# Order of the vector work in two attention layers: an eviction moved inside a head, copies, reciprocals and selection rounds moved between steps

## The reference

```python
# first layer, per block of 128 queries and head (16 heads of 64)
z = einsum(q, k) * scale
log_fail = where(mask, log_sigmoid(-z), 0.0)
later = cumsum(log_fail, reverse=True) - log_fail
a = where(mask, exp(log_sigmoid(z) + later), 0.0)
out = einsum(a, v)                      # then * silu(gate), @ w_out

# even layer: 8 heads of selected-key attention, 8 heads with three branches
rel = relu(einsum(q_idx, k_idx)); score = einsum(w_idx, rel)     # masked
_, idx = top_k(score, 128)              # topk = min(256, 512 // 4)
p = masked_softmax(einsum(q, k[idx]) * scale, valid)             # "d" units
# compressed keys ("c" units), selected blocks and window ("n" units)
o = g[..., 0] * o_c + g[..., 1] * o_s + g[..., 2] * o_w
```

## Time and profile before

| | |
|---|---|
| median of 3 runs | 2005.2 us (2001.36 to 2007.17) |
| the profiled execution | 2002.36 us, of it 2000.6 us span of the instructions |
| mean granted TensorE clock | 0.966 |
| PE busy (matmuls) | 1873.5 us, 94% |
| DVE, ACT, POOL busy | 49%, 40%, 24% |
| first layer's attention rounds | about 127 to 320 us |
| even layer: projections, then steps | about 616 to 732, 732 to 950 us |

### The profile page before, as it was taken

How to read it: one execution, slowest core, us unless ns; L and a number is a source line. 1 busy time by engine, 2 the same in 40 slices (tenths; PEclk the granted TensorE clock), 3 DMA queues, 4 the chain that set the end, 5 groups by cost and what they waited for, 6 DMA issues and landing times.

```text
span 2000.6 us, 24568 instructions
## 1 busy us (share of the span) xinstructions
PE 1873.5 (94%) x9662; PEld 1482.6 (74%) x9662; DVE 981.2 (49%) x1591; ACT 799.8 (40%) x1407; POOL 480.3 (24%) x478
## 2 busy tenths in 40 slices
PE   6999988997999889889999999999999899999997
PEld 5987776774577746656788888887877688888885
DVE  5345554587445566653543333355555454333334
ACT  4235554336434354435443233242444344332322
POOL 0035551000312344423021111003566302110100
PEclk9999999998999988979999999999999799999999
DMA  4321111221012410000233232222111023223232
GB/s 158 96 74 43 43 43 42 85 86 51 1 32 92 130 56 22 22 11 12 85 95 104 88 104 95 96 94 74 54 54 52 22 85 106 95 95 106 90 101 74
DMA packets 40289, 143.32 MB, mean 72 GB/s; under 512 B 4592, under 2 KB 4976, under 8 KB 40176
## 3 DMA queue, kind: packets, MB, share of 16 engines
q1 hardware_dynamic: 40176, 141.76, 21.9%
HBM read 139.64 MB, written 2.10 MB: 71 GB/s over the span
## 4 chain that ended last, share of the span: by engine, by line
PE 82%; DVE 8%; ACT 5%; issue 2%; POOL 2%; DMA 0%; DVEq 0%; SPq 0%; ACTq 0%; POOLq 0%
PE BANK L268 21%; PE BANK L270 21%; PE BANK L269 20%; PE BANK L832 2%; PE BANK L1458 1%; PE BANK L1415 1%; PE BANK L617 1%; DVE LH L703 1%; PE BANK L1439 1%; DVE SCR L698 1%; ACT WH L245 1%; PE BANK L886 1%; PE BANK L602 1%; PE BANK L2187 1%; PE BANK L2134 1%
## 5 line engine op out<-in xcount | busy, mean ns | idle before, releaser
L245 ACT ACTIVATE WH<-WRAW 128x1024 fp32r<-128x1024 f32 x262 | 273.3, 1045 | 473.6 <-PE BANK L270 430.9
L268 PE MATMUL BANK<-HH,WH 128*128 128x512 f32 x1048 | 428.1, 408 | 30.2 <-DVE WL L254 18.1
L254 DVE TENSOR_TENSOR WL<-WRAW,WH 128x1024 fp32r<-128x1024 f32 x242 | 318.9, 1318 | 255.2 <-ACT WH L245 255.0
L270 PE MATMUL BANK<-HL,WH 128*128 128x512 f32 x1048 | 412.1, 393 | 0.0
L269 PE MATMUL BANK<-HH,WL 128*128 128x512 f32 x1048 | 411.9, 393 | 0.0
L268 PEld LDWEIGHTS BANK<-HH,WH 128*128 128x128 f32 x1048 | 199.0, 190 | 80.9 <-issue 22.2
L269 PEld LDWEIGHTS BANK<-HH,WL 128*128 128x128 f32 x1048 | 199.0, 190 | 43.4 <-issue 5.3
L270 PEld LDWEIGHTS BANK<-HL,WH 128*128 128x128 f32 x1048 | 198.8, 190 | 42.7
L2075 POOL TENSOR_TENSOR HID<-TMP,HID 128x512 fp32r<-128x512 f32 x64 | 82.7, 1293 | 526.9 <-ACT HID L2056 526.9
L268 PE MATMUL BANK<-HID,WH 128*128 128x512 f32 x512 | 199.2, 389 | 0.0
L269 PE MATMUL BANK<-HID,WL 128*128 128x512 f32 x512 | 199.2, 389 | 0.0
(11 more groups left out here) (373 smaller groups left out, 3217.0 us busy)
## 6 DMA issues: line engine op xcount, KB each, us to landing
WRAW<-in_w SPq DMA_DIRECT2D x77, 512.0 KB, 3.4
WRAW<-in_wu SPq DMA_DIRECT2D x64, 512.0 KB, 3.3
WRAW<-in_wd SPq DMA_DIRECT2D x64, 512.0 KB, 3.3
WRAW<-in_w0o SPq DMA_DIRECT2D x8, 512.0 KB, 3.5
WRAW<-in_w1o SPq DMA_DIRECT2D x8, 512.0 KB, 3.4
WRAW<-in_wc SPq DMA_DIRECT2D x8, 512.0 KB, 3.3
WRAW<-in_w2o SPq DMA_DIRECT2D x8, 512.0 KB, 3.3
WRAW<-in_w3o SPq DMA_DIRECT2D x8, 512.0 KB, 3.4
```

Source lines behind the costliest of these rows:

```text
L245: e.activation(WH[b % NS][:, 0:n], WRAW[b % NR][:, 0:n], ACT.Copy).then_inc(*inc("s_high", ("high", b)))
L254: e.tensor_tensor(WL[b % NS][:, 0:n], WRAW[b % NR][:, 0:n], WH[b % NS][:, 0:n].bitcast(F32), ALU.subtract).then_inc(*inc("s_low_pool" if p ...
L268: e.matmul(dst, ah, bh, start=first and i == 0, stop=False)
L270: made = e.matmul(dst, ah, bl, start=False, stop=last and i == len(sets) - 1)
```

## The change

In the first layer `taken` is cut into `evicted` and `high`. The eviction of the first tile beside the heads stands behind the first cut of the second head's `fails`; `gated` goes behind that head, and the tile's high plane and the weight split behind `gated`. In the even layer four weight blocks (tiles 5 to 8) leave `on_pool` and are split by DVE. The rounds ahead of the steps are 5 + 5 instead of 4 + 3 + 3, and the third `index_sum` stands behind the eviction of tile 8. In the steps ACT copies ahead of the exponentials; reciprocals and scales come one step later; DVE's rope sum, ACT's high and POOL's low part of a turned tile come one step later, with POOL's cosine ahead of its scale. The rounds are one in a step in which a tile is turned, added or evicted and in every odd step, and two in the others; what is left is made in step 34.

```diff
-                   if block["e", 5] <= b <= block["e", 14] + NS and name not in ("wc1", "wc2")
+                   if block["e", 9] <= b <= block["e", 14] + NS and name not in ("wc1", "wc2")
...
             for m in range(8):
                 fails(2 * m)
+                fails(2 * m + 1, [0])
+                beside = l0_beside[m]
+                if len(beside) > 0:
+                    evicted(*beside[0])
+                fails(2 * m + 1, [1, 2])
                 if m:
                     gated(m - 1)
-                fails(2 * m + 1)
-                for t in l0_beside[m]:
-                    taken(*t)
+                if len(beside) > 0:
+                    high(*beside[0])
+                if len(beside) > 1:
+                    evicted(*beside[1])
+                    high(*beside[1])
...
             rounds = e_rounds(e, w)
-            for _ in range(4):
+            split("wc1", 1, 2)
+            for _ in range(5):
                 next(rounds)
-            split("wc1", 1, 2)
...
-            for _ in range(3):
+            for _ in range(5):
                 next(rounds)
             taken(E_Q)
             split("e", E_Q)
             after_rope(E_KW)
             keys(1)
-            index_sum(3)
             after_rope(E_Q)
-            for _ in range(3):
-                next(rounds)
             taken(E_Q + 1)
             split("e", E_Q + 1)
             c_keys(1)
             split("wc2", 1)
+            index_sum(3)
             for step in range(E_STEPS):
                 if 0 <= step - 1 < E_N:
                     maxima(step - 1)
-                if 0 <= step - 2 < E_N:
-                    recips(step - 2)
+                if 0 <= step - 3 < E_N:
+                    recips(step - 3)
...
+                if e_turning(step - 1) is not None:
+                    roped(e_turning(step - 1))
                 if e_turning(step) is not None:
-                    after_rope(e_turning(step))
+                    sines(e_turning(step))
...
-                next(rounds, None)
-                if step == e_first[4] - 3:
+                busy = [t for t in (e_turning(step - 1), e_turning(step), e_ended(step)) if t is not None]
+                for _ in range(1 if busy or step % 2 else 2):
+                    next(rounds, None)
+                if step == e_first[4] - 2:
                     for _ in rounds:
                         pass
...
             for step in range(E_STEPS):
-                if 0 <= step - 1 < E_N:
-                    exps(step - 1)
...
                 if 0 <= step - E_TURN < E_N:
                     copied(step - E_TURN)
-                if e_turning(step) is not None:
-                    high(e_turning(step))
+                if 0 <= step - 1 < E_N:
+                    exps(step - 1)
+                if e_turning(step - 1) is not None:
+                    high(e_turning(step - 1))
...
             gelu_low(1)
-            split("e", E_Q)
             cos(E_Q)
             low(E_Q)
+            split("e", E_Q)
             split("e", E_Q + 1)
             split("wc2", 1)
             w.wait_ge(*at("gates"))
             for step in range(E_STEPS):
-                if 0 <= step - 2 < E_N:
-                    scale(step - 2)
                 if e_turning(step) is not None:
                     cos(e_turning(step))
-                    low(e_turning(step))
+                if 0 <= step - 3 < E_N:
+                    scale(step - 3)
+                if e_turning(step - 1) is not None:
+                    low(e_turning(step - 1))
                 if e_ended(step) is not None:
                     split("e", e_ended(step))
```

More of the change, by code:

```diff
@@ L676, in l0_vector, with evicted @@
                 split_low(e, w, after_block(("l0v", b), 1), False)
-            def taken(name, m):
+            def evicted(name, m):
                 q = name == "l0q"
-                t = TMP[:, 2 + (not q), :]
                 w.wait_ge(*at("tile", name, m))
@@ L684, in taken, with high @@
                     w.wait_ge(*at("l0 low", name, m - 1))
-                e.scalar_tensor_tensor(out=t, in0=banks[name, m], scalar=0.125 if q else 1.0, in1=RS[:, :], op0=ALU.mult,
-                                       op1=ALU.mult).then_inc(*inc("s_evac", ("evac", name, m)))
+                e.scalar_tensor_tensor(out=TMP[:, 2 + (not q), :], in0=banks[name, m], scalar=0.125 if q else 1.0,
+                                       in1=RS[:, :], op0=ALU.mult, op1=ALU.mult).then_inc(*inc("s_evac", ("evac", name, m)))
+            def high(name, m):
+                q = name == "l0q"
                 w.wait_ge(*at("evac", name, m))
@@ L689, in taken, with fails @@
                     w.wait_ge(*at("z", 2 * m - 3, 2))
-                e.tensor_copy(l0_plane(m, 0 if q else 2), t).then_inc(*inc("s_l0_high", ("l0 high", name, m)))
+                e.tensor_copy(l0_plane(m, 0 if q else 2), TMP[:, 2 + (not q), :]).then_inc(
+                    *inc("s_l0_high", ("l0 high", name, m)))
                 split_low(e, w, after_block(name, m), False)
-            def fails(h):
+            def fails(h, ks=range(3)):
                 v = l0_buf[h % 3]
-                for k in range(3):
+                for k in ks:
                     c = cuts[k]
@@ L712, in gated @@
                     *inc("s_gated", ("gated", m)))
[L713 to L714 removed]
+            for t in l0_first:
+                evicted(*t)
+                high(*t)
             for m in range(8):
                 fails(2 * m)
+                fails(2 * m + 1, [0])
[3 more added lines that the diff above has]
+                fails(2 * m + 1, [1, 2])
                 if m:
                     gated(m - 1)
[L719 to L721 removed]
+                if len(beside) > 0:
[3 more added lines that the diff above has]
+                    high(*beside[1])
             gated(7)
@@ L1561, in after_rope, with sines @@
             def after_rope(t):
+                sines(t)
+                roped(t)
+            def sines(t):
                 w.wait_ge(*at("e rot", t))
```

1 line of the change is left out of this document (added).

## The result

The changed kernel takes **1978.2 us** (median of 4 runs, 1970.64 to 1981.56) against 2006.2 us (4 runs, 2001.36 to 2010.72) before: ratio 0.9855, 95% interval 0.9818 to 0.9893. Run again, beside 7 more runs of the kernel before, it gave 1977.5 us, ratio 0.9829 (0.9801 to 0.9857). The profiled execution took 1976.83 us, with 1975.0 us of span, at a mean granted clock of 0.970; the one of before took 2002.36 us.

What follows compares the result with a forecast made beforehand. Matmuls filled 94% of the span, leaving PE's idle and below-full-clock time to win. Terms -8.1 - 3.6 + 2.5 - 2.2 - 11.4 = -22.8 us gave 1979.6, or 1982 us on the median's footing; range 1974 to 1991.

Steps and rivals of the forecast that it cites:

- First layer, -8.1: First layer: five PE waits of 1.69 us for the eviction go, 0.3 us lost in the last round; -8.1 us.
- Head of the even layer, -3.6: Ahead of the steps: first scores 4.6 us sooner, some given back by the first turn; -3.6 us.
- `index_sum` and two rounds now lie ahead of the first maxima: Head of the even layer: one reason why part of the 4.6 us won at the first scores is given back.
- Turned tiles, +2.5: Steps: waits for cosine, scale and DVE, 15.7 us, replace 13.2 us of waits for copies; +2.5 us.
- The moved rope sum: Turned tiles: sum kept at 0.69 us; by the rule up to one `scale` lost at each of seven, 10 us.
- Late maxima, -2.2: Steps: at the 3.8 us wait, reciprocal and `scale` end near 848.0 instead of PE's restart at 850.12; -2.2 us.
- End of the selection, -11.4: Burst of rounds spread out: wait -6.3, lower clock behind it -4.6, shorter drop -0.5; -11.4 us.
- Rival 1: Turned tiles cost little: six waits of 2.5 us halve and the clock stays at 2.4 GHz; 1970 us, chance 0.15.
- rival 4: Nothing moves: first layer's wait goes over to `sums`, turned tiles eat the rest; 2000 to 2008 us, chance 0.08.
- Rival 3: Turned tiles: split, cosine and scale in line on GpSimd make waits of 5.1 us; 2016 us, chance 0.12.
- Rival 2: Steps 18 to 31: DVE becomes the bound through long rounds and the moved sum; 1994 us, chance 0.15.
- just fits: Steps: with reciprocals a step later, maxima, reciprocal and scale take 2.9 us against steps of 2.6 to 4 us.

Runs made afterwards that it cites:

- e1: The kernel before with only the first layer's part of the change; 1997.5 us, ratio 0.9942 to before.
- e6: The changed kernel with ACT's exponentials ahead of the copies again, as before the change; 1983.3 us, ratio 0.9884 to before.
- e4: The changed kernel with the third `index_sum` back ahead of the query's rope; 1971.2 us, ratio 0.9819 to before.
- e9: The changed kernel with reciprocals and scales a step sooner, third `index_sum` back, GpSimd's scale ahead of the cosine; 1945.8 us, ratio 0.9674 to before.
- e2: The changed kernel with the old order of the first layer, so only the even layer's part; 1988.3 us, ratio 0.9912 to before.
- e3: The changed kernel with GpSimd's scale ahead of the cosine in each step; 1966.1 us, ratio 0.9801 to before.
- e10: The kernel before with only the new pattern of selection rounds; 1997.3 us, ratio 0.9937 to before.
- e5: The changed kernel with one selection round a step and the rest at once in step 33; 1983.8 us, ratio 0.9879 to before.
- e7: The changed kernel with reciprocals and scales a step sooner, as before, cosine still ahead of scale; 1954.7 us, ratio 0.9739 to before.
- e11: The changed kernel with reciprocals and scales a step sooner and the third `index_sum` back; 1941.7 us, ratio 0.9647 to before.

## Why the prediction was right, and where it was not

The forecast of 1982 us lies 4 us over the result, and the range holds it. The nearness is partly luck: the trace has +8.1 us in the latent layer and -3.1 us behind the even layer, which no part of the forecast speaks of. The first layer's part came out 6.0 us larger than forecast. By its steps:

**First layer, -8.1: the mechanism right, the size too small, by a clock that the runs explain only in part.** The five waits are gone (8.5 us), and neither `sums`, `weigh` nor the weight load took them up. But the layer ends 14.1 us sooner, and 14.2 in e1. The other 5.6 us is the clock: at 127 to 178 and 178 to 277 us it was granted at 0.93 and 0.98 before, and 1.00 after. But only about 2 us of that (0.98 over 99 us) can belong to the evictions: the clock falls at 244 us, behind the fourth of the five waits (242.75). The 0.93 comes from one fall at 141 us, ahead of the first of them (170.26), behind a wait of 2.8 us of `sums` for GpSimd that stands in all three kernels below. At 140 to 150 us, in the kernel before, the changed one, and e6, whose first layer is the changed kernel's:

```profile
140.00:150.00 10.00, 9.95 (x39) 8.72 (x40) 5.64 (x8) 2.49 (x5) 5.50 (x4) 0.66 0.15 52
```

```profile
140.00:150.00 10.00, 9.51 (x57) 8.65 (x58) 5.87 (x9) 3.91 (x9) 6.10 (x5) 1.00 0.18 52
```

```profile
140.00:150.00 10.00, 9.18 (x37) 8.36 (x38) 6.17 (x9) 3.24 (x6) 6.38 (x5) 0.66 0.17 52
```

With this fall, e6 ends the first layer at 359.4, 9.6 us under before; without it, the changed kernel ends it at 354.8. e4 and e9, with a shorter fall there (0.97 at 127 to 178 us), end it at 357.6 and 357.4. On the other side e2, with the old order, has no fall there and still ends at 369.7, by falls elsewhere. So by all traces the new order is worth 9 to 16 us (353.6 to 359.4, against 368.6 to 369.7), of which 8.5 are the waits. What makes the clock fall behind the same wait in one kernel and not in another is open.

**Head of the even layer, -3.6: the first half right, the second wrong.** The scores started 5.9 us sooner by the stretch's own length (103.3 instead of 109.3 us; forecast 4.6). The one wait that was left is 3.8 us, as forecast under 4. The profile puts it down to "issue"; the last thing in front of it is GpSimd's low plane, which ends at 720.3. At the first turn (738.6 instead of 745.16) only 0.5 us of these 5.9 was left, the other 6.0 of its lead being older than the layer; the forecast kept 3.6. The step that failed is "`index_sum` and two rounds now lie ahead of the first maxima", which I walked at their undisturbed lengths. The sum's pair took 5.40 us beside GpSimd's splits, against 1.61, the first maxima came at 728.44, and PE waited 5.9 us for the exponentials. Of these, 2.7 us went with the sum in e4; the other 3.2 are ACT's weight block, whose load the walk left out. The row that warned of it was in the earlier trace rows, the rope sum of 2.78 us; I used it for the sum that the change moves in the steps, and not for the other sum of two SBUF operands that it moves next to splits.
The Trainium skill (SBUF — State Buffer, Who interferes with whom) says that a DVE instruction with two SBUF inputs contends with a GpSimd instruction that reads SBUF, and the trace agrees: 5.40 us beside the splits, 1.61 us away from them in e4.

**Turned tiles, +2.5: right.** I expected 15.7 us of waits for `scale` and for the compressed unit's weights from DVE; the trace has 14.3 + 2.4 = 16.7 us (1.0 us of it at 844.62 and 0.4 at 902.46, a step or more behind a turned tile), and at the tile of the earlier trace rows 3.44 us for a forecast of 2.5 + 1.0. These are the waits that the forecast named as its sign, and e3 shows the cause: changing the order of cosine and scale alone takes 7.8 us of these waits away.

**The moved rope sum.** It kept its 0.69 us on DVE in all seven tiles. It was GpSimd that paid:

```profile
756.44 1.30 POOL L1987 TENSOR_SCALAR SCR<-SCR,ST,enat 128x384 f32<-128x384 f32 x2
...
814.36 1.66 POOL L1987 TENSOR_SCALAR SCR<-SCR,ST,enat 128x384 f32<-128x384 f32 x2 [0.55 <-DVE ST L1671]
```

The second of these two ran with a rope sum beside it (814.17) and took 0.36 us more; at 784.17 four scales took 2.67 us, where two such pairs of the earlier trace rows make 2.18. So the price was 0.4 to 0.5 us at the tiles where the two met (five of the seven), not a whole `scale`.

**Late maxima, -2.2.** The turn at 850.12 comes at 844.62, and its lead grows from 2.7 us in the step before to 5.5: -2.8.

**End of the selection, -11.4.** No burst and no wait for a copy is left there. From the turn at 850.12 to that at 886.72 it is 36.6 us before and 23.1 after, -13.5 us, with a wait of 1.93 us for `scale` in it; from 850.12 to 892.04, the stretch by which e10 was read, it is 41.9 and 27.6, -14.3. The rounds alone gave -9.4 over that in e10, and the burst back cost 10.5 in e5. The forecast stands between these. One of its terms was read too small: at 873.93 to 886.72 us the granted clock was 0.55, which makes 11.5 us at the lower level and not 9.2. What I didn't see is that the pattern of rounds had a price of its own in the steps ahead (4.8 us in e10). That the copies' new place takes it away isn't shown: from the first scores to the turn at 850.12 it is 117.8 us before, 122.8 in e10, 124.2 in the changed kernel and 122.6 in e6, which has the old place of the copies. Only with the reciprocals back (e7) is it 105.6.

**Rivals.** Rival 1 (cheap turned tiles) and rival 4 (nothing moves) fell with the waits of 16.7 us and the first layer. Rival 3 was right in its mechanism, since the split, the cosine and the scale do stand in line, but the cosine starts 1.0 us after the rotation has ended at the tile of the earlier trace rows, not the 2.5 from which that rival decides, and the longest wait was 3.4 us. Rival 2 fell: DVE waited 38 us for scores ahead of its maxima in the steps.

**What the forecast didn't ask.** It took the reciprocals' later step as something that "just fits", and that is where the most time lay. e7 shows that this one part of the change costs 23 us of the median: the copies' waits went, and the scales' came in their place, for which only the later step was to blame. What helps in the even layer is the rest of the change. Its parts weren't all parted: no run has the early reciprocals with the exponentials ahead of the copies, and none puts back the moved weight splits or the later rope sum alone.

## What to carry to other kernels

When two waits stand in a chain (copy, then scale), taking slack from the second to free the first gives the gain back: change one, and leave the other its step. A wait of PE of 2 to 3 us is often worth more than its length here, since PE goes on at the lower clock behind it: in e7 16.7 us of waits gone made 25.0. Before a DVE instruction with two SBUF operands is moved, look at what GpSimd does at the new place. Beside a split of 2.34 us it was DVE that was stretched (2.78 us for 0.69, 5.40 for 1.61), beside a `scale` it was mostly GpSimd, even at 784.17, where `scale` had started 0.1 us ahead of the sum. If the stretched one is on the path to PE's next work, PE pays. And a split that comes later makes the next load into its buffer later, and with it what stands behind that block's high half on ACT (3.2 us of PE in e4).

## What the runs showed of the hardware

The latent layer, the same in all kernels, took 254.2 or 254.3 us in four traces (before, e5, e10, e11), 260.3 in e2 and 262.2 to 262.4 us in nine. PE's waits in it are much the same, 14 us in the kernel before and 13 in the changed one. In the changed kernel and in e11, at the same place within 1 us:

```profile
486.00:554.00 68.00, 68.00 (x310) 38.78 (x310) 27.97 (x100) 24.66 (x74) 20.30 (x32) 0.87 0.00 1
```

```profile
486.00:554.00 68.00, 67.69 (x353) 40.50 (x351) 31.76 (x114) 28.68 (x85) 23.73 (x37) 1.00 0.00 1
```

PE is busy throughout in both, but makes 310 matmuls at 0.87 in the first and 353 at 1.00 in the second. So 8 us of clock come and go in a stretch that no edit touches. Its cause is open and wasn't tried: e1 and e2, with each half of the change, both have the longer form. Each kernel but the changed one was traced once, so whether the form goes with the kernel or changes from run to run isn't shown; the four runs of e9, in two pairs 11 us apart, speak for the second. The fall of the clock at 141 us, there in e6 and not in the changed kernel, is of the same kind. A difference of under 10 us between two medians of this kernel is therefore read at the stretch that was edited, not at the total.
